# Five more tile pairs by seven products, value columns moved in between the attention parts, and a rotation that comes half a pair later

## The reference

```python
proj = h @ w_in                                  # 256 x 1024 by 1024 x 6622
fq, fk, fv | fox_f | dq, dk, dv | q_idx, k_idx, w_idx | sq, sk, sv | gates = split(proj)
o_fox = softmax attention with a decay from cumsum(log_sigmoid(fox_f + b))     # 6 heads of 64
dq, dk, q_idx, k_idx = rope(...)                                               # rotated
o_dsa = softmax attention over the 64 keys with the highest index score        # 5 heads
o_sb  = stick-breaking attention: exp(log_beta + reversed cumsum), masked      # 5 heads
g = sigmoid(gates)                                                             # 3 x 1024
merged = g0*(o_fox @ w_fox_out) + g1*(o_dsa @ w_dsa_out) + g2*(o_sb @ w_sb_out)
return merged @ w_out
```

## Time and profile before

| | |
|---|---|
| median of 3 runs | 2219.18 us (2218.52 to 2219.28) |
| profiled execution, its own time | 2218.83 us |
| span in it, first to last instruction | 2217.0 us |
| mean granted TensorE clock | 0.999 |
| PE busy | 2204.4 us (99%) |
| DVE busy | 1312.1 us (59%) |
| ACT busy | 547.8 us (25%) |
| DMA | 339.66 MB, mean 153 GB/s |

### The profile page before, as it was taken

How to read it: one execution, slowest core, us unless ns; L and a number is a source line. 1 busy time by engine, 2 the same in 40 slices (tenths; PEclk the granted TensorE clock), 3 DMA queues, 4 the chain that set the end, 5 groups by cost and what they waited for, 6 DMA issues and landing times.

```text
span 2217.0 us, 40707 instructions
## 1 busy us (share of the span) xinstructions
PE 2204.4 (99%) x16502; PEld 2074.7 (94%) x16502; DVE 1312.1 (59%) x2779; ACT 547.8 (25%) x1462; POOL 232.2 (10%) x405
## 2 busy tenths in 40 slices
PE   9999999999999999999999999999999999999998
PEld 9999998888999999999987899999889999889998
DVE  6775735533765666666373356664748763657764
ACT  2210333301221022003322022201415520334530
POOL 1110000000111011000000001100004420003430
PEclk9999999999999999999999999999999999999999
DMA  9656653443665556565434445556636545736652
GB/s 250 172 162 172 146 166 107 125 140 107 183 166 164 172 163 168 165 170 133 147 113 133 152 129 166 159 176 144 171 102 174 163 160 143 171 95 175 167 161 93
DMA packets 540164, 339.66 MB, mean 153 GB/s; under 512 B 45205, under 2 KB 533961, under 8 KB 539977
## 3 DMA queue, kind: packets, MB, share of 16 engines
q1 hardware_dynamic: 535248, 334.93, 53.2%
q10 hardware_dynamic: 4456, 1.08, 0.2%
q0 software_dynamic: 272, 1.05, 0.1%
HBM read 335.96 MB, written 1.05 MB: 152 GB/s over the span
## 4 chain that ended last, share of the span: by engine, by line
PE 87%; issue 7%; DVE 2%; POOLq 2%; POOL 1%; DVEq 1%; ACT 0%; DMA 0%; ACTq 0%; SPq 0%
PE bank L972 31%; PE bank L678 20%; PE bank L1050 15%; PE bank L746 6%; PE bank L687 4%; PE bank L1228 1%; PE bank L1219 1%; POOLq L1958 1%; POOL arena L1960 1%; PE bank L1321 1%; PE bank L1112 1%; PE bank L847 1%; POOLq L1975 0%; PE bank L1230 0%; PE bank L1061 0%
## 5 line engine op out<-in xcount | busy, mean ns | idle before, releaser
L972 PE MATMUL bank<-work,arena 128*128 128x128 f32 x2808 | 352.0, 275 | 0.1
L972 PEld LDWEIGHTS bank<-work,arena 128*128 128x128 f32 x2808 | 332.4, 192 | 0.3 <-ACT dmask L1721 0.3
L678 PE MATMUL bank<-hT,ring 128*128 128x256 f32 x1504 | 331.0, 380 | 0.0
L678 PEld LDWEIGHTS bank<-hT,ring 128*128 128x128 f32 x1504 | 283.9, 190 | 41.0 <-issue 2.7
L2001 DVE TENSOR_TENSOR arena<-ring 128x512 f32<-128x512 f32 (+1 forms) x378 | 257.7, 722 | 102.2 <-PE bank L1050 80.9
L972 PE MATMUL bank<-hT,ring 128*128 128x128 f32 x2128 | 281.1, 275 | 0.0
L972 PEld LDWEIGHTS bank<-hT,ring 128*128 128x128 f32 x2128 | 259.6, 192 | 0.4
L1050 PE MATMUL bank<-gates,arena 128*128 128x128 f32 x1536 | 211.1, 275 | 0.0
L1050 PEld LDWEIGHTS bank<-gates,arena 128*128 128x128 f32 x1536 | 190.8, 192 | 0.5
L1538 ACT ACTIVATE hT<-xT 128x512 f32<-128x512 f32 x48 | 29.7, 628 | 586.8 <-DVE xT L2004 562.1
L1903 POOL TENSOR_TENSOR small<-small 128x2 f32<-128x2 f32 x17 | 13.0, 763 | 1350.7 <-DVE small L1998 1134.9
(11 more groups left out here) (326 smaller groups left out, 2981.1 us busy)
## 6 DMA issues: line engine op xcount, KB each, us to landing
ring<-in_ffn_w_gu SPq DMA_DIRECT2D x174, 512.0 KB, 5.2
ring<-in_ffn_w_down SPq DMA_DIRECT2D x112, 512.0 KB, 4.5
ring<-in_ffn_w_up SPq DMA_DIRECT2D x84, 512.0 KB, 5.3
ring<-in_w_in SPq DMA_DIRECT2D x78, 512.0 KB, 5.2
ring<-in_w_in SPq DMA_DIRECT2D x26, 1024.0 KB, 5.3
ring<-in_w_out SPq DMA_DIRECT2D x16, 1024.0 KB, 5.0
ring<-in_ffn_w_down SPq DMA_DIRECT2D x32, 256.0 KB, 2.9
ring<-in_ca_w_kv SPq DMA_DIRECT2D x8, 1024.0 KB, 5.1
```

Source lines behind the costliest of these rows:

```text
L678: mm = pe.matmul(b[0:width, 0:S], view[:, c, a:a + width], src[:, c, :], start=(k == 0), stop=(k == C - 1))
L972: mm = pe.matmul(out_, a[:, c, :], b_[:, c, :], start=(start and c == 0), stop=(c == 3), skip_group_check=True)
```

## The change

The index key tile (`IK`) and gate tiles 0 to 8 join `PAIRS1`, which grows from 8 to 13 pairs: (ik, gate 0), then (1,2), (3,4), (5,6), (7,8). For gates DVE writes the sum into `gates` and raises `pair_staged`, and ACT takes the sigmoid in place. `LAST1` is gone. The plain gate tiles left are 9 and 10 (`GATES_A`), 11 to 17 (`GATES_C`), 18 to 23 (`GATES_D`). They are loaded as two DMAs of 128 columns for each slot instead of one of 256.

Two of the token slots (the DSA values, 160 columns wide each) move to the place of four of the six gate tiles after the stick-breaking products, and one (256 columns of the fox values) to the place of the four gate tiles after the decay sums. So the stretches between the attention parts become: 4 token tiles of width 160 and 2 gate tiles (was 6 gate tiles); 2 token tiles of width 256 (was 4); 7 gate tiles (was 8); 6 (as before).

In the pair loop, ACT exchanges the first tile of a pair in the next pair, after snap 2, and the second one after snap 3. DVE makes the sums first thing in each pair, from pair 0 on (before: pair 0 made none at its start and one at its end), rotates the first tile of the pair before between the two halves of this pair's first tile, and the second one at the start of the pair after. The sums' buffers move from `gates` to `work` and `oT`, which are free in the stage. The masks of `LS` and `zS` are applied only to the two of three 128-column blocks where the mask is not all ones. SP's order of loads follows.

```diff
-        mixer_sums = [cg(4, 512) for _ in range(3)]
+        mixer_sums = [cw(4, 512) for _ in range(2)] + [oT.rearrange("p (a b) s -> p a (b s)", b=2)]
...
-        PAIRS1 = list(zip(IQ, FK[1:3] + SQ)) + list(zip(DQ, SK)) + [tuple(DK), (DSQ, DSK)]
-        LAST1 = [("ik", 0, [(O_IK, HD), (O_IK, HD)])]
+        GATES = whole("gate", O_G, 24)
+        IK = ("ik", 0, [(O_IK, HD), (O_IK, HD)])
+        PAIRS1 = (list(zip(IQ, FK[1:3] + SQ)) + list(zip(DQ, SK)) + [tuple(DK), (DSQ, DSK), (IK, GATES[0])]
+                  + list(zip(GATES[1:9:2], GATES[2:9:2])))
+        GATES_A, GATES_C, GATES_D = ([GATES[a:min(a + 2, b)] for a in range(a0, b, 2)]
+                                     for a0, b in ((9, 11), (11, 18), (18, 24)))
+        TOK1_A, TOK1_B = [[(O_DV, 160, V_D)], [(O_DV + 160, 160, V_D + 160)]], [[(O_FV, 256, V_F)]]
...
         # PE, attention1
-                gate_tiles(6)
+                columns1(TOK1_A)
+                gate_tiles(GATES_A)
...
-                gate_tiles(4)
+                columns1(TOK1_B)
...
-                gate_tiles(8)
+                gate_tiles(GATES_C)
...
         # ACT, pairs1
-                        if k == 3:
-                            while waiting:
-                                exchange_staged(*waiting.pop())
+                        if k == 3 and waiting:
+                            finish(*waiting.pop(0))
...
-                    if names[0] in ROPED1:
-                        exchange_staged(q, 0, names[0])
-                    if names[1] in ROPED1:
-                        waiting.append((q, 1, names[1]))
+                    while waiting:
+                        finish(*waiting.pop(0))
+                    waiting += [(q, 0), (q, 1)]
...
         # DVE, proj1
-                    if waiting:
-                        rotate(*waiting.pop(0))
-                    if 0 < q < len(PAIRS1) - 2:
+                    for tile in late:
+                        rotate(*tile)
+                    if q < len(PAIRS1) - 2:
                         make_sums()
-                    if waiting:
-                        rotate(*waiting.pop(0))
...
                     stt(d0[:, P:S], rc, s0, keep[:, 2, :], ALU.mult, ALU.add)
+                    for tile in waiting[0:1]:
+                        rotate(*tile)
+                    late = waiting[1:]
                     v.wait_ge(sem["product_done"], p0 + 6)
...
-                    if q == 0:
-                        make_sums()
...
         # DVE, mixer1
+                columns1(TOK1_A)
                 v.wait_ge(sem["softplus_out"], n("softplus_out"))
...
-                tt(LS[:, :, :], LS[:, :, :], strict, ALU.mult).then_inc(sem["operand_ready"], 1)
+                tt(masked(LS), masked(LS), strict, ALU.mult).then_inc(sem["operand_ready"], 1)
...
-                tt(zS[:, :, :], zS[:, :, :], strict, ALU.mult).then_inc(sem["operand_ready"], 1)
+                tt(masked(zS), masked(zS), strict, ALU.mult).then_inc(sem["operand_ready"], 1)
+                columns1(TOK1_B)
```

More of the change, by code:

```diff
@@ L578, in _ @@
                     ld.cols(io["w_in"], l, tile_parts(tiles), ("product_done", 7))
[L579 to L580 removed]
+                for cols in TOK1 + TOK1_A:
                     ld.cols(io["w_in"], l, tok_parts(cols), ("proj_done", T))
[L582 to L583 removed]
+                for tiles in GATES_A:
+                    ld.cols(io["w_in"], l, tile_parts(tiles), ("gate_done", len(tiles)))
+                for cols in TOK1_B:
+                    ld.cols(io["w_in"], l, tok_parts(cols), ("proj_done", T))
+                for tiles in GATES_C + GATES_D:
+                    ld.cols(io["w_in"], l, tile_parts(tiles), ("gate_done", len(tiles)))
                 for m in range(0, C, 2):
@@ L820, in proj1, with columns1 @@
                 banks.set_free([(b, None) for b in (0, 1)]
[L821 to L824, removed]
+                               + [(b, ("pair_read", all_read - k)) for k in (1, 0)
+                                  for b in SETS[(len(PAIRS1) - k) % 2]])
+            def columns1(columns):
+                for cols in columns:
+                    tokens(len(cols), sum(w for _, w, _ in cols), hT)
             def tokens(loads, width, src, kind="proj_done", releaser="dve_released"):
@@ L832, in tokens, with gate_tiles @@
                     tok(b, t, view, width, src).then_inc(sem[kind], 1)
-            def gate_tiles(count):
-                for _ in range(count // 2):
-                    view, loaded = slots.next(1)
+            def gate_tiles(slots_):
+                for tiles in slots_:
+                    view, loaded = slots.next(len(tiles))
                     view = view.rearrange("p (c n) -> p c n", n=S)
                     pe.wait_ge(*loaded)
-                    for j in range(2):
+                    for j in range(len(tiles)):
                         b = free("gate_done", "act_released")
@@ L1479, in _ @@
                 proj1()
-                for cols in TOK1:
-                    tokens(len(cols), sum(w for _, w, _ in cols), hT)
+                columns1(TOK1)
                 attention1()
@@ L1594, in pairs1, with finish @@
                 waiting = []
-                def exchange_staged(q, j, name):
-                    act.wait_ge(sem["pair_staged"], n("pair_staged"))
-                    exchange(staged(q, j), ROPED1[name], xr)
+                def finish(q, j):
+                    name, i, _ = PAIRS1[q][j]
+                    if name in ROPED1:
+                        act.wait_ge(sem["pair_staged"], n("pair_staged"))
+                        exchange(staged(q, j), ROPED1[name], xr)
+                    elif name == "gate":
+                        act.wait_ge(sem["pair_staged"], n("pair_staged"))
+                        act.activation(gates[:, i, :], gates[:, i, :], ACT.Sigmoid)
                 for q, tiles in enumerate(PAIRS1):
@@ L2419, in proj1, with rotate @@
                 make_sums()
-                waiting = []
-                def rotate(b, name, i, in_bank=False):
+                waiting, late = [], []
+                def rotate(b, name, i):
                     w = ROPED1[name]
@@ L2455, in proj1 @@
                     ts(d1[:, 0:P], ra, s1, None, ALU.mult).then_inc(sem["pair_read"], 1)
-                    if r1:
+                    if r1 or tiles[1][0] == "gate":
                         v.drain().then_inc(sem["pair_staged"], 1)
@@ L2459, in proj1, with columns1 @@
                     n("snapped", 4)
-                    if q == 0:
-                        make_sums()
[L2462 to L2467, removed]
+                    waiting = [(staged(q, j), name, i) for j, (name, i, _) in enumerate(tiles) if name in ROPED1]
+            def columns1(columns):
+                for cols in columns:
+                    for t in range(T):
+                        v.wait_ge(sem["proj_done"], n("proj_done"))
+                        b = seen("dve", "proj_done")
+                        a = 0
+                        for _, w, c in cols:
+                            ins = v.tensor_copy(vtok[:, t, c:c + w], b[:, a:a + w])
+                            a += w
+                        ins.then_inc(sem["dve_released"], 1)
             def less_max(p, t, heads, w):
@@ L2499, in decay_sums_kept, with masked @@
                  .then_inc(sem["dve_released"], 1)
+            def masked(p):
+                return p.rearrange("p h (a b) -> p h a b", b=P)[:, :, 0:3:2, :]
             def mixer1(l):
                 proj1()
[L2503 to L2511, removed]
+                columns1(TOK1)
                 v.drain()
```

30 lines of the change are left out of this document (14 added, 16 removed).

## The result

The changed kernel takes 2206.93 us (median; 2206.49 to 2207.09), the kernel before 2218.78 us beside it (2218.25 to 2219.28): a ratio of 0.9946, interval 0.9933 to 0.9959, 11.85 us less. The profiled execution took 2207.03 us, its span is 2205.2 us against 2217.0, and its granted clock 0.999.

A forecast was written before the change was run, and what follows sets the result against it. PE was taken to bound the kernel (87% of the span). A layer gains 3.40 + 2.68 - 0.2 - 0.1 = 5.8 us, two layers 11.6: 2207.6 us from the median 2219.18, range 2206.2 to 2210.8.

The forecast's parts named there:

- Ten tiles in five pairs: Index key tile and nine gate tiles as five pairs: PE time from 34.7 to 31.3 us, gain 3.40 a layer.
- The ring: ACT and DVE's exchange, rotation, sums and tile, 6.43 us against PE's 6.255 a pair; removing its waits gains 2.68 less 0.2.
- the long stall: PE's 1.67 us stall in the mixer's pairs, read as the ring once with two sets of sums in it.
- The table load: ACT's table switch at the first sigmoid, in pair 9: hidden, cost 0; without cover at most 1.3 us.
- Cover before `LS`: PE's shorter work before `LS`, 15.65 us instead of 20.82: PE waits 0 to 0.1, taken as 0.1 a layer.
- `zS`, fox and DSA: Covers before `zS` and the fox and DSA probabilities: no PE wait, cost 0; `zS` has 4 us spare.
- Token tiles cost the same wherever they stand: Token tiles moved between the attention parts: PE's time for them unchanged, cost 0.
- Weights' ring: Rival, slower (0.02): thirteen pairs outrun the weight loads, 6.9 us a pair, and 26 pairs lose 16.6 us.
- weight loads in the open: Rival (0.01): a pair's 24 more weight loads cannot run beside matmuls, 4.6 us more a pair; kernel near 2250.
- the ring stays: Rival (0.15): snap 3 or DVE's wait between the halves keeps pairs waiting; 2209 to 2210.5, or 2212.4 with all 2.68 lost.

The follow-up runs named there:

- the full mask: The changed kernel with both masks (`LS` and `zS`) over all 1920 columns again: 2208.27 us, ratio 0.9953.
- the old order: The changed kernel with exchanges, rotations and sums in the order of the kernel before; thirteen pairs, token tiles and masks stay: 2220.50 us, ratio 1.0007.
- the kernel with the token tiles ahead: The changed kernel with the three moved token slots put back ahead of attention: 2237.22 us, ratio 1.0084.

## Why the prediction was right

2207.6 against 2206.93, and 11.6 us of span against 11.8. The time counted from a median before of 2219.18; beside the changed kernel the one before took 2218.78, which is why 2206.93 lies below the 2207.0 that was the most the rows allowed. The gain itself, 11.85 us, is within the 12.2. By its own steps:

- *Ten tiles in five pairs, 3.40 a layer.* Right, a little more: thirteen pairs take 81.29 us, and thirteen times the feed-forward's 6.255 is 81.3, while PE's time on plain tiles in the mixer falls from 86.8 us (25 tiles) to 52.0 (15), 34.8 for the ten.
- *The ring, 2.68 less 0.2.* The 2.68 is right, and shown alone by the kernel before with the new order (5.4 us in two layers). The 0.2 was not needed: no pair waits. The working behind it holds to hundredths: snap 3 ends at 5.18 in the pair, 5.15 forecast. DVE was less late than worked out, 1.8 and 2.8 us behind pairs 8 and 9 instead of 2.4 and 3.6. Its reading of the long stall as two sets of sums in one turn of the ring is half of it: with one set the stall is 0.79, and with the exchange moved the second set costs nothing.
- *The table load, 0.* Right. Sigmoid done at 297.63, 6.9 us from the start of pair 9 at 290.73 (6.83 forecast). The Trainium skill, "ScalarE: Activation LUTs", section "What ACT_TABLE_LOAD costs", would have had it 1.38 us later; the sigmoid starts 1.29 us after the load does, so this trace has no such drain.
- *Cover before `LS`, 0.1.* A little too dear: PE does not wait, and by the full mask it has 0.26 us left. The four token copies were put 0.3 us ahead of the softplus. The last ends at 339.89 and the softplus at 339.94 (338.14 + 1.80, its ACT row): 0.05, hidden but only just.
- *`zS`, fox and DSA, 0.* Right, with 4.2, 6.0 and 5.6 us to spare in the first layer by DVE's and PE's rows. Forecast were 4, 6 and 2, the last without any gain of the chain on DVE and ACT.
- *Token tiles cost the same wherever they stand, 0.* Nearly. In three stretches they take 12.65 + 8.80 + 7.09 = 28.54 us of PE a layer, where in one they took 319.11 - 290.85 = 28.26: 0.28 more.
- *Weights' ring and weight loads in the open, rivals at 2%, 1%.* Neither. The pairs keep 6.253 us.

So 3.40 + 2.68 = 6.08 was the most, 5.96 a layer came, 5.8 was forecast. That it came so near is in small part luck: the 0.3 us a layer put against the gain did not come, and 0.28 came at a term that was put at 0.

One thing would have failed had it been asked: the rival *the ring stays*, priced at 2209 to 2212.4. The run nearest to it, the old order in this stage, takes 2220.5, outside the range. The price came from eight pairs, of which the last two have two rotated tiles each and make no sums. In thirteen the sums go on there.

## What to carry to other kernels

When two engines feed each other round a third, look for the operation that stands just ahead of the first result the bound engine waits for, and move it to where the slack is; measured apart, that move, the exchange with its rotation, was all of the reordering's worth (5.4 us in the two stages), and making the sums earlier added nothing to it. Price a ring in the stage as it will be, pair by pair, with all the work that meets in each: a ring that cost 2.7 us a layer in eight pairs cost 5.9 in thirteen, and 7.6 where the clock fell as well. And work that covers another engine's chain pays for being made cheaper only as far as other work takes its place: without it the same gates in pairs made this kernel 0.8% slower than the one before.

## What the runs showed of the hardware

A stall of TensorE costs more than its length when the granted clock falls behind it. It was 0.50 (1.2 GHz) after idle times of 8.26 and 2.83 us, and once after 2.05 us, for 3.3 to 4.6 us in which PE worked; after 2.04 us, in that last kernel's first layer, and after 1.67 us it stayed 1.00. That cost 7.5 us in the kernel with the token tiles ahead and 1.6 in the one with the old order. And a small activation between two others on ACT delayed the next one's start by 0.11 us, not by the 0.21 of its record, because its record and the next one's overlap (252.67 + 0.21 against 252.79).
